# The last two output pairs in stretches of 384 and 136 tokens instead of 260 and 260

## What is computed

```python
    hn = rmsnorm(h, norm_ffn)
    h = h + (jax.nn.silu(hn @ w_ff_gate) * (hn @ w_ff_up)) @ w_ff_down
...
y_prompt = rmsnorm(hp, norm_final)
y_sample = rmsnorm(hs, norm_final)
...
def rmsnorm(x, g):
    x32 = x.astype(jnp.float32)
    y = x32 * lax.rsqrt(jnp.mean(x32 * x32, axis=-1, keepdims=True) + EPS)
    return y.astype(x.dtype) * g
```

## Time and profile before

| | us |
|---|---|
| median of 3 runs | 1070.36 (1070.26 to 1071.53) |
| the profiled execution: its time | 1069.9 |
| its span in the trace | 1068.1 |
| PE busy | 1057.1 (99%) |
| PEld busy | 1050.2 (98%) |
| DVE busy | 717.6 (67%) |
| ACT busy | 479.8 (45%) |
| POOL busy | 110.9 (10%) |
| matmuls, and weight loads | 8751 each |

### The profile page before, as it was taken

How to read it: one execution, slowest core, us unless ns; L and a number is a source line. 1 busy time by engine, 2 the same in 40 slices (tenths; PEclk the granted TensorE clock), 3 DMA queues, 4 the chain that set the end, 5 groups by cost and what they waited for, 6 DMA issues and landing times.

```text
span 1068.1 us, 20525 instructions
## 1 busy us (share of the span) xinstructions
PE 1057.1 (99%) x8751; PEld 1050.2 (98%) x8751; DVE 717.6 (67%) x1234; ACT 479.8 (45%) x550; POOL 110.9 (10%) x93
## 2 busy tenths in 40 slices
PE   9999999999999999999999999999999999999997
PEld 8999999999999999999999999999999999999996
DVE  6766677888888654686323755578778457588754
ACT  6744343453335353344345823344456245366431
POOL 4671000002300000000000000000000000000000
PEclk9999999999999999999999999999999999999999
DMA  8967886789796878558876663231588366487512
GB/s 297 283 186 191 222 212 150 195 229 316 213 271 143 207 184 215 149 150 192 205 188 158 159 237 117 80 97 43 150 193 191 112 147 147 119 198 182 164 40 80
DMA packets 151193, 187.25 MB, mean 175 GB/s; under 512 B 4758, under 2 KB 141294, under 8 KB 145590
## 3 DMA queue, kind: packets, MB, share of 16 engines
q1 hardware_dynamic: 117894, 106.93, 31.7%
q0 software_dynamic: 8496, 57.15, 26.7%
q10 hardware_dynamic: 24720, 21.97, 6.7%
HBM read 122.34 MB, written 7.54 MB: 122 GB/s over the span
## 4 chain that ended last, share of the span: by engine, by line
PE 95%; DVE 2%; DMA 1%; ACT 1%; ACTq 0%; POOL 0%; issue 0%; DVEq 0%; POOLq 0%
PE acc L2173 39%; PE acc L2191 20%; PE acc L2545 12%; PE acc L2499 11%; PE acc L2506 6%; PE acc L2284 1%; PE acc L2145 1%; PE acc L2388 1%; PE acc L2364 1%; DMA w_raw<-in_w_v_dram 1%; PE acc L2292 1%; DVE o_acc L1603 0%; POOL w_l L699 0%; PE acc L2277 0%; DVE ubyb L1434 0%; ACTq L758 0%
## 5 line engine op out<-in xcount | busy, mean ns | idle before, releaser
L2173 PE MATMUL acc<-big_h,w_h 128*128 128x260 f32 x1664 | 336.6, 283 | 0.1
L2173 PE MATMUL acc<-big_l,w_h 128*128 128x260 f32 x1664 | 334.2, 282 | 0.0
L2173 PEld LDWEIGHTS acc<-big_h,w_h 128*128 128x128 f32 x1664 | 255.8, 188 | 0.7 <-DVE st L1639 0.3
L2173 PEld LDWEIGHTS acc<-big_l,w_h 128*128 128x128 f32 x1664 | 256.2, 188 | 0.0
L2191 PE MATMUL acc<-big_h,w_l 128*128 128x260 f32 x1664 | 209.0, 282 | 0.0
L2191 PEld LDWEIGHTS acc<-big_h,w_l 128*128 128x128 f32 x1664 | 203.7, 188 | 0.2 <-DMA w_l<-w_raw 0.2
L1434 DVE SCALAR_TENSOR_TENSOR ubyb<-ubyb,prm 128x512 f32<-128x512 f32 (+1 forms) x240 | 180.3, 751 | 15.2 <-DVE ubyb L1434 9.4
L725 ACT ACTIVATE w_h<-w_raw 128x1024 fp32r<-128x1024 f32 x120 | 120.2, 1052 | 100.2 <-DMA w_raw<-in_w_out_a_dram 29.4
L2499 PE MATMUL acc<-x_h,ws_h 128*128 128x260 f32 x504 | 125.8, 282 | 0.0
L2499 PE MATMUL acc<-x_l,ws_h 128*128 128x260 f32 x504 | 125.7, 282 | 0.0
L2499 PEld LDWEIGHTS acc<-x_h,ws_h 128*128 128x128 f32 x504 | 94.8, 188 | 0.3 <-ACT cp L1164 0.2
(11 more groups left out here) (277 smaller groups left out, 1325.8 us busy)
## 6 DMA issues: line engine op xcount, KB each, us to landing
w_l<-w_raw POOLq DMA_DIRECT2D x41, 1024.0 KB, 8.1
w_raw<-in_w_in_dram SPq DMA_DIRECT2D x36, 1024.0 KB, 5.1
ws_l<-w_raw POOLq DMA_DIRECT2D x18, 768.0 KB, 6.9
w_raw<-in_w_ff_gate_dram SPq DMA_DIRECT2D x18, 512.0 KB, 4.8
w_raw<-in_w_ff_up_dram SPq DMA_DIRECT2D x18, 512.0 KB, 4.9
k_st<-in_cache_mem_k_dram ACTq DMA_DIRECT2D x8, 1024.0 KB, 8.9
v_st<-in_cache_mem_v_dram ACTq DMA_DIRECT2D x8, 1024.0 KB, 12.8
w_raw<-in_w_v_dram SPq DMA_DIRECT2D x4, 1024.0 KB, 8.1
```

Of the source, the lines that this page charges most:

```text
L2173: last = M.matmul(out[:, b, 0:HALF], w_h[:, slot, k, cols], xs[:, k_at + k, b * HALF:(b + 1) * HALF], start=start and k == 0 and xs is x[0 ...
```

## The change

- `STRETCHES` = (0, 384), (384, 520): pairs 2 and 3 are computed, added, squared and summed for tokens 0 to 383 first, then for the other 136 (tokens 384 to 511 and the samples). The number of matmuls doesn't change. Pairs 0 and 1 stay as they are.
- `GROUPS`: the first group of rows is t = 0, 1, 2, the second t = 3 and the samples (called 4). Where the flips land in PSUM changes with that (`ROWS_AT`); the sums of the two groups go to other banks (`SUMS_AT`), so a wait for `y_step` stands ahead of the products that reuse the bank.
- The part of the second group's sum over tokens t = 3 that comes from the first seven tiles' squares (`AHEAD`, source `hs`) is issued before the last 8 products, behind a wait for `y_hs`.
- The refinement is written in four steps behind the root instead of five; the product with -0.5 is made before the root is there.
- Scaling: DVE takes t = 0 and half of t = 2 in the first group, and t = 3 in two halves in the second; ACT takes t = 1 and half of t = 2, then the samples.
- SP stores t = 0, t = 1, t = 2 in halves, and t = 3 in halves; ACT issues the store of the samples itself.

```diff
+STRETCHES = ((0, 384), (384, 520))
+GROUPS = ((0, 1, 2), (3, 4))
+SCALE_DVE = (((0, 0, D), (2, 0, D // 2)), ((3, 0, D // 2), (3, D // 2, D)))
+SCALE_ACT = (((1, 0, D), (2, D // 2, D)), ((4, 0, D),))
+ROWS_AT = {(0, 4): (((2, 0, 0), (0, 1)), ((2, 1, 0), (2,))), (0, 6): (((3, 0, 0), (0, 1)), ((3, 1, 0), (2,))),
+           (1, 4): (((2, 0, 1), (3,)), ((2, 1, 1), (4,))), (1, 6): (((3, 0, 0), (3,)), ((2, 1, 0), (4,)))}
+SUMS_AT = ((3, 0, 1), (2, 0, 0))
+COLUMN = (0, 1, 2, 3, 4)
+AHEAD = (3,)
...
@@ sync
+            for scaled, count, piece in ((y_dve, 1, SCALE_DVE[0][0]), (y_act, 1, SCALE_ACT[0][0]),
+                                         (y_dve, 2, SCALE_DVE[0][1]), (y_act, 2, SCALE_ACT[0][1]),
+                                         (y_dve, 3, SCALE_DVE[1][0]), (y_dve, 4, SCALE_DVE[1][1])):
                 sp.wait_ge(scaled, count)
+                sp.dma_start(rows_in_memory(piece), scaled_rows(piece)).then_inc(y_out, 16)
-            sp.wait_ge(y_dve, 4)
-            sp.dma_start(y_sample.rearrange("s t d -> (s t) d"), ys_st[:, :]).then_inc(y_out, 16)
...
@@ scalar
-                act.wait_ge(refined, 20 + 5 * part_n)
+                act.wait_ge(refined, 19 + 4 * part_n)
+                for piece in SCALE_ACT[part_n]:
+                    scaled, r = scaled_rows(piece), row_scale(piece[0])
+                    nc.scalar.activation(scaled, scaled, ACT.Copy, scale=r).then_inc(y_act, 1)
+            act.wait_ge(y_act, 3)
+            act.dma_start(rows_in_memory(SCALE_ACT[1][0]), scaled_rows(SCALE_ACT[1][0])).then_inc(y_out, 16)
...
@@ vector
 last_add:
+                a, e = STRETCHES[b]
-                    V.tensor_tensor(h_sb[:, n, toks], acc[down_slot(p, j)][:, b, 0:HALF], h_sb[:, n, toks], ALU.add) \
+                    V.tensor_tensor(h_sb[:, n, a:e], acc[down_slot(p, j)][:, b, 0:e - a], h_sb[:, n, a:e], ALU.add) \
...
+            def last_scale(b):
+                cols = slice(GROUPS[b][0], GROUPS[b][-1] + 1)
+                less, t, r = ssy[:, 6 + cols.start:6 + cols.stop], t_[:, cols], rfin[:, cols]
+                dve.wait_ge(y_step, b + 1)
+                V.tensor_scalar(less, ssy[:, cols], -0.5, None, ALU.mult).then_inc(y_less, 1)
+                dve.wait_ge(y_root, b + 1)
+                step(V.reciprocal(r, r))
+                step(V.tensor_tensor(t, r, r, ALU.mult))
+                dve.wait_ge(y_less, b + 1)
+                step(V.tensor_tensor(t, t, less, ALU.mult))
+                step(V.scalar_tensor_tensor(r, t, 1.5, r, ALU.add, ALU.mult))
+                for piece in SCALE_DVE[b]:
+                    scaled, scale = scaled_rows(piece), row_scale(piece[0])
+                    V.tensor_scalar(scaled, scaled, scale, None, ALU.mult).then_inc(y_dve, 1)
...
@@ tensor
 products:
-                                last = M.matmul(out[:, b, 0:HALF], w, inner(kind[1], k, b),
+                                a, e = stretches[b]
+                                last = M.matmul(out[:, b, 0:e - a], w, inner(kind[1], k, a, e),
...
 (last_products is products for one stretch b of STRETCHES, all k)
             last_flips(6, 0)
             last_flips(7, 0)
-            last_sums(0, 2, 8, 6)
-            products(s2, (0, 1), (1,), all_k, LOW, end=True, low_done=d_full)
-            products(s3, (0,), (1,), all_k, HIGH, begin=True)
-            products(s3, (0,), (1,), all_k, LOW, end=True, low_done=d_full)
+            pe.wait_ge(y_hs, 6)
+            pe.wait_ge(y_sq, 8)
+            for t, n in itertools.product(GROUPS[0], range(2)):
+                last = last_sum(0, t, n)
+            last.then_inc(y_sums, 1)
+            last_products(s2, (0, 1), 1, LOW, end=True, low_done=d_full)
+            pe.wait_ge(y_step, 1)
+            last_products(s3, (0,), 1, HIGH, begin=True)
+            last_products(s3, (0,), 1, LOW, end=True, low_done=d_full)
             last_flips(4, 1)
             last_flips(5, 1)
-            products(s3, (1,), (1,), all_k, HIGH, begin=True)
+            last_products(s3, (1,), 1, HIGH, begin=True)
             last_flips(6, 1)
-            products(s3, (1,), (1,), all_k, LOW, end=True, low_done=d_full)
+            pe.wait_ge(y_hs, 9)
+            for t in AHEAD:
+                last_sum(1, t, 0)
+            last_products(s3, (1,), 1, LOW, end=True, low_done=d_full)
             last_flips(7, 1)
-            last_sums(2, 3, 12, 9)
+            pe.wait_ge(y_sq, 12)
+            for t in AHEAD:
+                last_sum(1, t, 1)
+            for n in range(2):
+                last = last_sum(1, 4, n)
+            last.then_inc(y_sums, 1)
```

More of the change, by code:

```diff
@@ L523, in own, with last_bank, scaled_rows, row_scale @@
             return i * (2 * per_pass) + 2 * (offset - OWN + 1)
[L525 to L529, removed]
+        def last_bank(place):
+            p, j, bank = place
+            return acc[down_slot(p, j)][:, bank, :]
+        def scaled_rows(piece):
+            t, a, e = piece
+            return y_st[:, t, a:e] if t < 4 else ys_st[:, a:e]
+        def row_scale(t):
+            return rfin[0:P if t < 4 else TS, COLUMN[t]:COLUMN[t] + 1]
+        def rows_in_memory(piece):
+            t, a, e = piece
+            return y_prompt[0, t * P:(t + 1) * P, a:e] if t < 4 else y_sample.rearrange("s t d -> (s t) d")[:, a:e]
         def first_use(s):
@@ L1211, in _ @@
             nc.scalar.activation(t_[:, 0:1], t_[:, 1:2], ACT.Sqrt).then_inc(table_loaded, 1)
-            for part_n, (a, b, r) in enumerate(((0, HALF, 1), (HALF, TOK, 3))):
+            for part_n, (a, b) in enumerate(STRETCHES):
                 for n in range(4, KT):
@@ L1215, in _ @@
                     nc.scalar.activation(sq4[:, n - 4, a:b], h_sb[:, n, a:b], ACT.Square).then_inc(y_sq, 1)
-                cols = slice(0, 2) if part_n == 0 else slice(2, 5)
+                cols = slice(GROUPS[part_n][0], GROUPS[part_n][-1] + 1)
                 act.wait_ge(y_step, part_n + 1)
                 nc.scalar.activation(rfin[:, cols], ssy[:, cols], ACT.Sqrt).then_inc(y_root, 1)
-                act.wait_ge(refined, 20 + 5 * part_n)
-                for half in range(part_n + 1):
-                    scaled = y_st[:, r, half * D // 2:D if part_n == 0 else (half + 1) * D // 2]
-                    nc.scalar.activation(scaled, scaled, ACT.Copy, scale=rfin[:, r:r + 1]).then_inc(y_act, 1)
+                act.wait_ge(refined, 19 + 4 * part_n)
[4 more added lines that the diff above has]
+            act.dma_start(rows_in_memory(SCALE_ACT[1][0]), scaled_rows(SCALE_ACT[1][0])).then_inc(y_out, 16)
         @block.vector
@@ L2080, in last_sum @@
                 nonlocal sums
-                toks = slice(b * HALF, (b + 1) * HALF)
+                toks = slice(*STRETCHES[b])
                 dve.wait_ge(y_sq, 4 * b + n + 1)
@@ L2090, in last_rows @@
                 c = slice(n0 * P, (n0 + 2) * P)
[L2091 to L2109, removed]
+                for place, ts in ROWS_AT[b, n0]:
+                    if ts == (4,):
+                        V.tensor_tensor(ys_st[:, c], last_bank(place)[0:TS, 0:2 * P], gfin[0:TS, c], ALU.mult)
+                        continue
+                    count = len(ts)
+                    V.tensor_tensor(y_st[:, ts[0]:ts[0] + count, c],
+                                    last_bank(place)[:, 0:count * 2 * P].rearrange("p (t c) -> p t c", t=count),
+                                    gfin[:, c].rearrange("p (t c) -> p t c", t=1).broadcast_to([P, count, 2 * P]), ALU.mult)
@@ new lines, in last_mean @@
+            def last_mean(b):
+                cols = slice(GROUPS[b][0], GROUPS[b][-1] + 1)
+                dve.wait_ge(y_sums, b + 1)
+                V.tensor_scalar(ssy[:, cols], last_bank(SUMS_AT[b])[:, cols], 0.0, EPS, ALU.max, ALU.add).then_inc(y_step, 1)
+            def last_scale(b):
+                cols = slice(GROUPS[b][0], GROUPS[b][-1] + 1)
+                less, t, r = ssy[:, 6 + cols.start:6 + cols.stop], t_[:, cols], rfin[:, cols]
[10 more added lines that the diff above has]
+                    V.tensor_scalar(scaled, scaled, scale, None, ALU.mult).then_inc(y_dve, 1)
@@ L2119, in _ @@
             last_rows(0, 6)
-            last_mean(0, slice(0, 2))
-            last_scale(0, slice(0, 2))
+            last_mean(0)
+            last_scale(0)
             last_add(2, 1)
@@ L2126, in _ @@
             last_rows(1, 6)
-            last_mean(1, slice(2, 5))
-            last_scale(1, slice(2, 5))
-            V.tensor_scalar(ys_st[:, :], ys_st[:, :], rfin[0:TS, 4:5], None, ALU.mult).then_inc(y_dve, 1)
+            last_mean(1)
+            last_scale(1)
         @block.tensor
@@ L2517, in rows_out, with inner, products @@
                     flip(rows[0:TS, 1, 0:P], h_sb[:, n, TP:TOK]).then_inc(acc_done, 1)
[L2519 to L2524, removed]
+            def inner(part_x, k, a, e):
+                return mid[:, k // 2, part_x, k % 2 * TOK + a:k % 2 * TOK + e]
+            EVEN = ((0, HALF), (HALF, TOK))
```

(28 more changed lines are left out.)

9 lines of the change are left out of this document (3 added, 6 removed).

## The result

The changed kernel takes 1074.68 us in the median of 13 executions (1072.28 to 1080.64), the kernel before beside it 1070.73 of 13 (1069.62 to 1071.96): slower by 4.0 us from median to median. The ratio that is given with its interval, 1.0045 (1.0031 to 1.0059), is that of all executions together, whose means are 1075.5 and 1070.8. The forecast was 1073.6, a ratio of 1.0030. The 13 executions aren't one group. Eight lie between 1072.28 and 1074.71 us with a mean granted clock of 0.997 to 0.999, five between 1077.5 and 1080.64 with 0.991 or 0.992, and none between. The profiled execution (1078.67 us, span 1076.9, clock 0.992) is of the second group.

What follows compares the result with a forecast made beforehand. TensorE, busy 99% of the span, was taken to bound the kernel, then a serial tail of 9.1 us. Terms: 4.8 + 0.8 - 0.7 - 0.2 - 1.4 = +3.3 us, forecast median 1073.6, range 1070.0 to 1075.2.

Steps and rivals of the forecast that it cites:

- 384-column product: First-stretch products of pairs 2 and 3: 175 ns each by the slope from 260 to 512 columns, bounds 172 and 179.
- 136-column product: Second-stretch products of pairs 2 and 3: 116 ns each because the weight load decides, bounds 109 and 120.
- last add later than in the earlier trace: Sign in the trace after: the last add comes about 5.6 us later than 1058.97.
- last add to scaling: Serial tail: -0.7 us from last add to mean with 136 columns, -0.2 us for one refinement step fewer.
- scaling to end of span: Scaling and stores: fewer bytes left to store after the second scaling, 3.9 us instead of 5.4, -1.4 us.
- The added waits: TensorE's waits for `y_step` and for `y_hs` 9: cost 0, the first with 1.4 us of margin.
- rival 3: One of the two added TensorE waits comes late by about 1 us: 1074.6; chance 0.11 together with rival 4.
- rival 4: Samples' store by ACT lands last, stores save 0.1 instead of 1.4 us: 1074.9; chance 0.11 together with rival 3.
- rival 1: Loads of fp32r weights hide, so a 136-column product costs 62 ns: 1068.5 us; chance 0.14.
- rival 2: Short fp32r products stream at a slower rate, 232 ns for 136 columns: 1084.8 us in all; chance 0.05.
- the case that was forecast: Main case: load-bound short products outweigh the shorter tail, +3.3 us, median 1073.6 us; chance 0.70.
- The sum of the lowest terms: All terms at their low end: +1.8 us, or 1072.2 us; at the other end +4.5, or 1074.9.

Runs made afterwards that it cites:

- a0_after: The changed kernel again with no edit, six executions, all with the clock held: 1074.23 us, ratio 1.0033; the one profiled took 1072.86 us.
- a2_after: The changed kernel again with no edit, eight executions, four held and four with fallen clock: 1076.28 us, ratio 1.0050.
- even_tail_new: Changed kernel with stretches of 260 and 260 and the earlier row groups; four-step refinement and samples' store on ACT's queue kept: 1069.97 us, ratio 0.9997.
- few_sums: Changed kernel with 2 instead of 6 row sums in the first group, leaving out the sums of tokens 128 to 383: 1073.11 us, ratio 1.0018.
- mixed: Changed kernel with the 32 high 136-column products of s2 alternating with 384-column ones: 1073.89 us, ratio 1.0042, one of six fell.
- w192: Changed kernel with second-stretch products streaming 192 instead of 136 columns, only the last 136 used: 1073.21 us, ratio 1.0028; again 1073.42 us, 1.0025.
- w256: Changed kernel with second-stretch products streaming 256 instead of 136 columns, only the last 136 used: 1073.31 us, ratio 1.0025.
- short64: Kernel before with the 96 second-stretch products of pairs 2 and 3 streaming 64 columns, tokens 324 to 519 left out: 1077.01 us, ratio 1.0068.

## Why the prediction was right and wrong

**Right: the terms, with the clock held.** Against the execution a0_after, which held its clock (span 1071.1, +3.0 beside the 1068.1 of before):

| step | forecast | measured |
|---|---|---|
| 384-column product | 175 ns | 11.20/64 = 175 ns |
| 136-column product | 116 ns (109 to 120) | (6.34 - 16 x 0.175 + 4.53 + 1.74 + 0.97)/96 = 112 ns |
| last add later than in the earlier trace rows | +5.6 us | 1064.24 - 1058.97 = +5.3 |
| last add to scaling | -0.9 us | 2.70 for 3.70: -1.0 |
| scaling to end of span | -1.4 us | 1071.1 - 1066.9 = 4.2 for 5.4: -1.2 |

The added waits cost nothing, since TensorE has no gap at either (against rival 3). The span ends 3.0 us after ACT issues the samples' store (1068.12 us), where rival 4 had 3.7 and 0.4. Rivals 1 and 2 are refuted: the loads don't hide (192 columns cost what 136 and 64 cost), and short fp32r products have no slower rate. 22 of 33 executions are the case that was forecast, at +3.4 for +3.3 us. The sum of the lowest terms was +1.9, not +1.8, which changes nothing.

The rule of the Trainium skill that the time between matmuls is N/2.4 + 2.5 ns ("TensorE: Matmul & The Clock Gate", section "Back-to-back issue gap") doesn't describe this kernel: 59 ns for 136 columns, 112 measured. The section itself gives it for a matmul without the time of its load and calls it too short for small N, which the prediction left out. The Trainium skill's rule for the load (same page, section "LDWEIGHTS (loading the stationary operand)"), 107 ns for 128 columns, comes close for these products. It doesn't hold for the float32 flips of the earlier trace rows, 62 ns each with 128 columns loaded, though the prediction says that its rows agree.

**Wrong: the clock.** The step that failed is the sentence under "What bounds the kernel now" that the clock is 2.4 GHz in all slices "and nothing here leaves it idle long enough to change that". Idleness was the wrong thing to look for. TensorE, shown as busy for 1.00 of 1 us before, during and after the fall, lost half its clock in 11 of 33 executions, amid load-bound products, flips and sums. The forecast had the ingredients: it put a 136-column product at 116 ns, where its own rival 1 has 62 for streaming 136 columns, but took the difference only as time. What the fall costs, from the two profiled executions: from the start of the 64 products to the last add +5.0 us (1069.77 - 1036.57 = 33.20 for 1064.24 - 1036.07 = 28.17), the two flips, the six sums and the steps up to the scaling +0.3 (2.95 for 2.70), in all 5.3. The other 0.5 us of the difference in span (1076.9 - 1071.1) is older than the fall. Between the medians of the two groups lie 4.7 us. No rival had it, and neither of the two signs of being wrong that the prediction names came: no product took below 100 ns, and TensorE didn't stand still.

The median of the first 13, 1074.68, is close to the forecast partly by luck. With five fallen of 13 the median is still a held execution; with four of eight, in a2_after, it is 1076.28. The mean of the 13 is 1075.5, and a third of all executions lie above 1077, while the range ended at 1075.2.

The Trainium skill's table in "Why this matters for your kernels", on the same page, ties such a drop to gaps in which TensorE is idle; this trace doesn't agree, as it shows no gap ahead of 1059 us.

**What is shown and what is open.** Shown: the loss is the split's, with its groups (even_tail_new); 3.4 us of it, with the clock held, is the length of the short, load-bound products and the added sums, less the shorter tail; the rest is the clock. Beside the changed kernel on the same chips the clock held with 192 columns streamed in place of 136 at the same length of product (0 of 18 for 6 of 14) and, less surely, with fewer one-column matmuls (few_sums, 0 of 11 for 4 of 8). In the order of the kernel before, which never lost it, it fell with 64 columns (5 of 5) and with 136 and 16 more sums (5 of 5). Open: why one execution of the same kernel falls and the next doesn't, and whether the chip has a part in how often; what the flips do, which no run varied; whether 136 columns alone can bring the clock down in the order of before; and whether breaking up the short products helps (mixed).

No version beat the kernel before. Of the complete kernels with this split the best are w192 (1.0028 and 1.0025) and w256 (1.0025), and they do more arithmetic than the change.

## What to carry to other kernels

Where each matmul loads its own 128 columns of 4-byte weights, it costs about 110 ns here however short its stream; an uneven split of the moving columns then loses on its short side, and the short side can be widened at hardly any cost while the load is the longer (to 192 columns in this kernel; 256 cost 0.7 us). A TensorE that is shown busy all the time lost its clock all the same: give a run of load-bound matmuls, flips and one-column sums a rival of its own, priced at the lower clock. A spread of execution times that appears with a change is a finding; sort the executions by their mean clock before taking a median.

## What the runs showed of the hardware

- The granted clock fell from 1.00 to 0.50 with TensorE shown busy for all of the stretches before (1050 to 1059 us in the changed kernel).
- At the lower clock a load-bound product takes twice as long: 16 products of 136 columns take 3.31 us, 207 ns each, for 1.74, 109 each. With 64 columns it is 203 ns (3.25/16, short64), so there too the length doesn't follow the stream. That the load of the weights itself slows with the granted clock is inferred from this.
- fp32r products with their own load, at the full clock: 64 columns 109 ns, 136 columns 112, 192 columns 113 (the mean of the same 96 products), 256 columns 121 (4.83/40), 260 columns 120, 384 columns 175, 512 columns 232.
